# An FFN down projection on seven block products: one core, fp32 in three fp32r passes

## The reference, cut to what matters

```python
D_MODEL = 2048;  D_FF = 4 * D_MODEL;  SEQ = 512;  DEC_BATCH = 8   # 520 tokens reach the FFN
h = _rms_norm(x, g_ffn)
u = jnp.square(jax.nn.relu(jnp.einsum('bld,df->blf', h, w_up)))
return x + jnp.einsum('blf,fd->bld', u, w_down)
```

## Time and profile before

| what | us |
|---|---|
| median of three runs | 3292.89 |
| span of the profiled execution | 3293.0 |
| TensorE busy | 3158.8 (96%) |
| VectorE busy | 1949.6 (59%) |
| ScalarE busy | 1439.7 (44%) |
| first matmul of the up projection | at 1860.09 |
| last product of the up projection | at 2527.92 |
| last addition to xd | at 3287.26 |

### The profile page before, as it was taken

How to read it: one execution, slowest core, us unless ns; L and a number is a source line. 1 busy time by engine, 2 the same in 40 slices (tenths; PEclk the granted TensorE clock), 3 DMA queues, 4 the chain that set the end, 5 groups by cost and what they waited for, 6 DMA issues and landing times.

```text
span 3293.0 us, 66551 instructions
## 1 busy us (share of the span) xinstructions
PE 3158.8 (96%) x24759; PEld 3020.4 (92%) x24759; DVE 1949.6 (59%) x2700; ACT 1439.7 (44%) x1998; POOL 342.2 (10%) x623
## 2 busy tenths in 40 slices
PE   6999999999999999899889699999999999999999
PEld 6999999999999998775389699999999999999999
DVE  4225666665555558899843687887876333433333
ACT  4224666665555556677722344444443122121211
POOL 1111111111111113233300000000000000000000
PEclk9999999999999999999999899999999999999999
DMA  6434333333343338799953244444445323333322
GB/s 186 114 107 110 102 97 99 106 101 93 108 114 93 106 96 297 270 362 326 377 188 102 90 129 128 128 132 135 135 134 191 128 93 115 115 117 122 120 90 91
DMA packets 506127, 472.92 MB, mean 144 GB/s; under 512 B 19680, under 2 KB 435312, under 8 KB 504856
## 3 DMA queue, kind: packets, MB, share of 16 engines
q1 hardware_dynamic: 465616, 353.80, 36.1%
q0 software_dynamic: 40416, 117.93, 10.4%
HBM read 426.85 MB, written 44.80 MB: 143 GB/s over the span
## 4 chain that ended last, share of the span: by engine, by line
PE 88%; DVE 6%; DMA 3%; ACT 1%; issue 1%; POOL 0%; SPq 0%; POOLq 0%; ACTq 0%; DVEq 0%
PE ps L901 26%; PE ps L902 26%; PE ps L903 26%; PE ps L1084 3%; PE ps L1095 2%; PE ps L1096 2%; PE ps L1017 2%; DMA pg<-in_cache_fox_v_dram 1%; DVE pg_lo L1773 1%; PE ps L1127 1%; PE ps L1126 1%; PE ps L948 1%; DMA x2T<-xT_dram 0%; DVE qp_lo L1773 0%; DVE w_lo L1773 0%
## 5 line engine op out<-in xcount | busy, mean ns | idle before, releaser
L901 PE MATMUL ps<-h_hi,w_hi 128*128 128x260 f32 (+1 forms) x2592 | 750.0, 289 | 16.1 <-DVE h_lo L1773 13.0
L902 PE MATMUL ps<-h_hi,w_lo 128*128 128x260 f32 (+1 forms) x2592 | 737.3, 284 | 0.0
L903 PE MATMUL ps<-h_lo,w_hi 128*128 128x260 f32 (+1 forms) x2592 | 736.5, 284 | 0.0
L1773 DVE TENSOR_TENSOR w_lo<-w_raw,w_hi 128x2048 fp32r<-128x2048 f32 (+1 forms) x241 | 466.8, 1937 | 275.4 <-ACT w_hi L1323 239.6
L1323 ACT ACTIVATE w_hi<-w_raw 128x2048 fp32r<-128x2048 f32 x160 | 305.9, 1912 | 693.0 <-PE ps L903 680.1
L901 PE MATMUL ps<-ub_hi,w_hi 128*128 128x260 f32 x2048 | 581.6, 284 | 9.9 <-DVE xd L2184 5.5
L903 PE MATMUL ps<-ub_lo,w_hi 128*128 128x260 f32 x2048 | 580.4, 283 | 0.0
L902 PE MATMUL ps<-ub_hi,w_lo 128*128 128x260 f32 x2048 | 580.2, 283 | 0.0
L901 PE MATMUL ps<-b_hi,w_hi 128*128 128x260 f32 x1792 | 508.3, 284 | 29.6 <-DVE b_lo L1773 25.2
L901 PEld LDWEIGHTS ps<-h_hi,w_hi 128*128 128x128 f32 x2592 | 491.4, 190 | 19.6 <-DVE h_lo L1773 14.5
L902 PE MATMUL ps<-b_hi,w_lo 128*128 128x260 f32 x1792 | 508.3, 284 | 0.0
(11 more groups left out here) (303 smaller groups left out, 5160.4 us busy)
## 6 DMA issues: line engine op xcount, KB each, us to landing
w_raw<-in_w_in_dram SPq DMA_DIRECT2D x81, 1024.0 KB, 5.7
w_raw<-in_w_down_dram SPq DMA_DIRECT2D x64, 1024.0 KB, 5.4
w_raw<-in_w_up_dram SPq DMA_DIRECT2D x32, 1024.0 KB, 8.3
x2T<-in_w_up_dram SPq DMA_DIRECT2D x64, 512.0 KB, 5.4
pg<-in_cache_sb_v_dram POOLq DMA_DIRECT2D x106, 256.0 KB, 4.9
w_raw<-in_cache_fox_k_dram SPq DMA_DIRECT2D x72, 256.0 KB, 5.4
u_dram<-x2T SPq DMA_DIRECT2D x64, 260.0 KB, 3.0
u_st<-u_dram SPq DMA_DIRECT2D x8, 2080.0 KB, 7.8
```

The costliest lines, as they stand in the source:

```text
L901: pe.matmul(out, whi, xhi, start=first, stop=False, skip_group_check=more)
L902: pe.matmul(out, wlo, xhi, start=False, stop=False, skip_group_check=more)
L903: return pe.matmul(out, whi, xlo, start=False, stop=last, skip_group_check=more)
L1773: return dve.tensor_tensor(out, a, hi.bitcast(F32), ALU.subtract)
```

## The change

The down projection gets the same form as the up projection. NC becomes 4 chunks of KF = 8 pairs of u tiles (16 k-tiles); within a chunk there are 8 pairs (q) of output tiles, each with seven block products of 24 matmuls. Pairs are numbered through, 0 to 31 up and 32 to 63 down (`Pair`), and `weights`, `high`, `low`, `weight_sum` and `product` serve both.

- The seven token blocks of the down projection are no longer formed from u by itself: the up projection computes them per pair (u11, u21 and u22 themselves, and t5 = u12 - u11, t6 = u22 - t5, u22 - u12, t4 = u21 - t6: four more VectorE additions of 128x260 a pair), keeps them in u7 (two buffers in x2T), and POOL stores all seven slices (910 KB) to u_dram, which is now 7 x 128 x 32 x 260.
- At a chunk's end POOL loads block i (1040 KB, 8320 B a partition) into b_raw, which lies over b_lo, as soon as product i+1 of the chunk's last pair is done; ScalarE (`block_high`) and VectorE (`block_low`) split it in place. Blocks 0 to 3 are split within the last pair of a chunk, 4 to 6 within the first pair of the next.
- Weight blocks: a11, a12 and a21 have one buffer each now, in w_raw, and a22 two (one over the attention masks). SP loads each as 512 KB when the low part that reads it last is done.
- In the down projection VectorE adds the seven banks to xd (`add`, one of them to three quarters of the pair at once: 780 columns with the bank broadcast).
- xd lies where x2T was; SP loads tiles 0 to 3 early, POOL tiles 4 to 15 after the last store of u.
- The results are turned in place: `turn` (8 transposes of the pair before, into banks 6 and 7) and `turn_samples` (2) stand between the products of the last chunk's pairs, ScalarE copies back to xd, SP stores from there. yn goes.

The diff, cut to its core:

```diff
-S_WO, S_FF = 81, 97
-FC = 1024
-NC = FF // FC
+S_WO = 81
 NU = FF // (2 * P)
-KF = FC // P
+KF = 8
+NC = NU // KF
...
-        u_dram = nc.dram_tensor("u_dram", [FF // P, P, TQ], F32).ap()
+        u_dram = nc.dram_tensor("u_dram", [7, P, NU, HQ], F32).ap()
...
+        b_raw = at("b_raw", [P, 7, KT // 2, HQ], F32, HALF)
+        xd = at("xd", [P, KT, TQ], F32, at_r)
+        u7 = [x2T[:, 8:15, HQ * i:HQ * i + HQ] for i in range(2)]
+        u_p1, u_p16, u_p165 = (x2T[:, k, 0:HQ] for k in (7, 6, 5))
+        assert odd_at + 4096 <= late0
+        a22_odd = nc.alloc_sbuf_tensor_at("a22_odd", [P, KT // 2, P], F32, offset=odd_at)
+        a11, a12, a21 = w_raw[0][:, 0:8, :], w_raw[0][:, 8:16, :], w_raw[1][:, 0:8, :]
+        a22 = [w_raw[1][:, 8:16, :], a22_odd[:, :, :]]
...
+            def weights(g, b11, b12, b21, b22):
+
+                wait(sp, a_lo, count(g, 7, -7))
+                sp.dma_start(a22[g.p], b22).then_inc(a22_ld[g.p], 16)
+                wait(sp, a_lo, count(g, 7, -5))
+                sp.dma_start(a11, b11).then_inc(a11_ld, 16)
+                wait(sp, a_lo, count(g, 7, -2))
+                sp.dma_start(a21, b21).then_inc(a21_ld, 16)
+                wait(sp, a_lo, count(g, 7, -1))
+                sp.dma_start(a12, b12).then_inc(a12_ld, 16)
...
+            def store(g):
+                pool.wait_ge(r_ok, count(g, 2, 2))
+                pool.wait_ge(u_ok, count(g, 3, 3))
+                pool.wait_ge(t_ok, count(g, 4, 4))
+                dst = u_dram[:, :, g.n:g.n + 1, :] if not g.mult else u_dram[:, :, bass.ds(g.x * 2 + g.n, 1), :]
+                pool.dma_start(dst.rearrange("s p o t -> p s (o t)"), u7[g.p]).then_inc(u_sv[g.p], 16)
+
+            def block_load(g, c, i):
+
+                pool.wait_ge(p_ok, count(g, 7, i + 1))
+                src = u_dram[i, :, bass.ds(c * KF, KF), :] if not isinstance(c, int) else u_dram[i, :, c * KF:c * KF + KF, :]
+                pool.dma_start(b_raw[:, i, :, :], src).then_inc(blk_ld[i], 16)
+
+            for p in range(2):
+                store(Pair(p))
+            with pool.Fori(1, NU // 2 - 1) as j:
+                for p in range(2):
+                    store(Pair(p, j, 2))
+            pool.wait_ge(u_sv[0], 64)
+            pool.wait_ge(u_sv[1], 64)
+            for i in range(7):
+                block_load(Pair(NU - 1), 0, i)
+                if i == 0:
+                    store(Pair(NU - 2))
+            store(Pair(NU - 1))
+            pool.wait_ge(x2_sw, 16)
+            for p in range(2):
+                pool.wait_ge(u_sv[p], 8 * NU)
+            pool.dma_start(xd[:, 4:KT, :], x2_dram[:, 4:KT, :]).then_inc(xd_ld[1], 16)
+            with pool.Fori(0, NC - 1) as c:
+                for i in range(7):
+                    block_load(Pair(NU + KF - 1, c, KF), c + 1, i)
...
+            def down(g, fresh=None, turned=None):
+
+                a, b, c = g.p, 2 + g.p, 4 + g.p
+                if g.q == 1:
+                    pe.wait_ge(r_ok, 2 * NU)
+                    pe.wait_ge(c_ev, 5 * NU)
+                pe.wait_ge(e_ok, count(g, 7, -14 + 3))
+                product(g, 1, a, True, False, fresh)
+                pe.wait_ge(e_ok, count(g, 7, -14 + 6))
+                product(g, 6, b, True, False, fresh)
+                pe.wait_ge(e_ok, count(g, 7, 1))
+                product(g, 2, a, False, False, fresh)
+                if turned is not None:
+                    turn(turned)
+                pe.wait_ge(e_ok, count(g, 7, 2))
+                product(g, 5, b, False, False, fresh)
+                pe.wait_ge(e_ok, count(g, 7, -14 + 7))
+                product(g, 7, c, True, False, fresh)
+                if turned is not None:
+                    turn_samples(turned)
+                pe.wait_ge(e_ok, count(g, 7, 4))
+                product(g, 3, b, False, False, fresh)
+                pe.wait_ge(e_ok, count(g, 7, 5))
+                product(g, 4, c, False, False, fresh)
...
+            def block_high(c, i):
+                act.wait_ge(blk_ld[i], count(c, 16, 32))
+                act.activation(b_hi[:, i, :, :], b_raw[:, i, :, :], ACT.Copy).then_inc(blk_hi, 1)
...
+            def down(g, nxt, old=None, new=None, done=None):
+                high(g, 7)
+                if old is not None:
+                    block_high(old, 4)
+                high(g, 3)
+                if old is not None:
+                    block_high(old, 5)
+                if new is not None:
+                    block_high(new, 0)
+                high(g, 4)
+                if old is not None:
+                    block_high(old, 6)
+                if new is not None:
+                    block_high(new, 1)
+                if done is not None:
+                    turned(done)
                 if nxt is not None:
...
+                    high(nxt, 5)
+                    high(nxt, 1)
+                if new is not None:
+                    block_high(new, 2)
+                if done is not None:
+                    turned_samples(done)
+                if nxt is not None:
+                    high(nxt, 6)
+                if new is not None:
+                    block_high(new, 3)
+                if nxt is not None:
+                    high(nxt, 2)
+
...
+            def block_low(c, i):
+                dve.wait_ge(blk_hi, count(c, 7, i + BLK0 + 1))
+                minus(b_lo[:, i, :, :], b_raw[:, i, :, :], b_hi[:, i, :, :]).then_inc(blk_lo, 1)
...
                 low(g, 3)
-                if nxt is not None:
-                    first_sums(nxt)
+                low(g, 4)
+                weight_sum(nxt, 1)
                 dve.wait_ge(p_ok, count(g, 7, 4))
-                dve.tensor_tensor(u_p165[:, :], u_p1[:, :], b, ALU.add).then_inc(c_ev, 1)
-                low(g, 4)
-                if nxt is not None:
-                    low(nxt, 5)
-                    second_sum(nxt)
+                dve.tensor_tensor(u_p165, u_p1, b, ALU.add).then_inc(c_ev, 1)
+                if new is not None:
+                    block_low(new, 0)
+                weight_sum(nxt, 2)
+                low(nxt, 5)
                 dve.wait_ge(p_ok, count(g, 7, 5))
                 dve.wait_ge(c_ev, count(g, 5, 2))
-                wait(dve, u_sv[p], count((g[0], 0), 16, 0))
-                dve.tensor_tensor(u22, u_p165[:, :], c, ALU.add).then_inc(c_ev, 1)
+                wait(dve, u_sv[g.p], count2(g, 16, 0))
+                dve.tensor_tensor(u22, u_p165, c, ALU.add).then_inc(c_ev, 1)
+                low(nxt, 1)
+                relu_square(u22, 3)
+                if new is not None:
+                    block_low(new, 1)
+                weight_sum(nxt, 3)
+                dve.wait_ge(p_ok, count(g, 7, 6))
+                dve.tensor_tensor(u12, u_p1, b, ALU.add).then_inc(c_ev, 1)
+                low(nxt, 6)
+                relu_square(u12, 4)
+                dve.wait_ge(r_ok, count(g, 2, 2))
+                dve.wait_ge(u_ok, count(g, 3, 2))
+                dve.tensor_tensor(t5, u12, u11, ALU.subtract).then_inc(t_ok, 1)
+                if new is not None:
+                    block_low(new, 2)
+                dve.wait_ge(p_ok, count(g, 7, 7))
+                dve.tensor_tensor(u21, u_p16, c, ALU.add).then_inc(c_ev, 1)
+                dve.wait_ge(t_ok, count(g, 4, 1))
+                dve.tensor_tensor(t6, u22, t5, ALU.subtract).then_inc(t_ok, 1)
+                dve.tensor_tensor(u12, u22, u12, ALU.subtract).then_inc(t_ok, 1)
+                low(nxt, 2)
+                relu_square(u21, 5)
+                weight_sum(nxt, 4)
+                dve.wait_ge(u_ok, count(g, 3, 3))
+                dve.wait_ge(t_ok, count(g, 4, 2))
+                dve.tensor_tensor(t4, u21, t6, ALU.subtract).then_inc(t_ok, 1)
+                if new is not None:
+                    block_low(new, 3)
+
+            last = NU // 2 - 1
+            up(Pair(0), Pair(1), TOKENS[4:])
+            up(Pair(1), Pair(2))
+            with dve.Fori(1, last) as j:
+                up(Pair(0, j, 2), Pair(1, j, 2))
+                up(Pair(1, j, 2), Pair(2, j, 2))
+            up(Pair(NU - 2), Pair(NU - 1))
+            up(Pair(NU - 1), Pair(NU), (), Pair(0))

+            def down(g, nxt, old=None, new=None):
+                m = 2 * g.q
+                a, b, c = (ps[:, r + g.p, 0:HQ] for r in (0, 2, 4))
+                x11, x12, x21, x22 = (xd[:, m + i, h * HQ:(h + 1) * HQ] for i in range(2) for h in range(2))
+                x3 = xd[:, m:m + 2, :].rearrange("p m t -> p (m t)")[:, HQ:4 * HQ].rearrange("p (o t) -> p o t", o=3)
+
+                def add(n, x, bank, before=None):
+                    dve.wait_ge(p_ok, count(g, 7, n))
+                    if before is not None:
+                        dve.wait_ge(e_ok, count(g, 7, before))
+                    dve.tensor_tensor(x, x, bank, ALU.add).then_inc(e_ok, 1)
+
+                if g.q in (0, 2):
+                    dve.wait_ge(xd_ld[g.q // 2], 32 if g.q == 0 else 64)
```

(76 more changed lines are left out.)

461 lines of the change are left out of this document (158 added, 303 removed).

## The result

The changed kernel takes **3332.7 us** (median of 4 runs, 3323.82 to 3341.66) against 3292.98 for the kernel before on the same chip: a ratio of 1.012, 95% interval 1.0097 to 1.0143. It is slower by 40 us, where 3251 was forecast and 3280 was the top of the range. The profiled execution, from which all rows of this kernel come, is the longest of the four: 3341.66 us, span 3340.1. The four lie 18 us apart, those of the kernel before 5.

A forecast was written before the change was run, and what follows sets the result against it. TensorE, busy 96% of the span, was taken as the bound. From the 3293.0 us span, -94.4 - 13.8 - 2.5 + 15 + 37 + 17 = -41.7 gave 3251 us, range 3208 to 3280.

The forecast's parts named there:

- the ring: Up projection: VectorE's chain from first sum to low 7, 15.2 us plus a21's landing, costs nothing up to 4.9 us landing.
- -94.4: Down projection on TensorE: 6144 matmuls (737.9 us) become 5376 (643.5 us), saving 94.4 us.
- -13.8: Passage from up to down: the idle time and slow clock around the store-reload of the last u values go, saving 13.8 us.
- -2.5: Start of the up projection: TensorE's wait for eviction c2 shrinks as loads start earlier, saving 2.5 us, bounds 0 and -6.
- the fourth case: Up projection: VectorE saturates through more dependent waits, 1 us a pair, 3283 us; chance 0.20 together with the late-blocks rival.
- I take the median, 5.4: Up projection: a21 assumed to land in 5.4 us beside the store, costing 0.5 us x 31 pairs, +15 us.
- The third case: Up projection: a21 lands behind the store at 8.1 us, pairs take 23.3 us, 3335 us in all; chance 0.10.
- the ring in the down projection: Down projection: VectorE's chain closing on the a21 load takes 13.5 us, with no store beside it, so costs 0.
- The walk that gave 12.3 us: Chunk boundaries: stepping through late additions behind block work, TensorE loses 12.3 us at each of three boundaries.
- 37 + 17: Boundary costs: +37 us for three chunk boundaries, +17 us for the passage from up to down.
- The second case: Boundaries: blocks land late, boundaries 16.5 and passage 25 us, 3272 us, up to 3290 with late weights; chance 0.20 with VectorE saturation.
- the bare balance of 6.3 each: Chunk boundaries: VectorE's work over two pairs, 46.5 us against 40.2, a bare excess of 6.3 us.

The follow-up runs named there:

- late-stores version: Changed kernel, but POOL's store of a pair's seven slices waits until the a21 load two pairs ahead has landed: 3263.84 us.
- the gates on the weight loads: Late stores and reordered boundaries, plus block 1 sent only after a21 landed and block 2 only after a12: 3244.49 us.
- the new order: Late stores, plus block 0 rounded after high 4, later blocks one step later, block 3 in the next chunk, additions 4 and 5 earlier: 3255.71 us.
- the last three moves: On the gated version: a store behind all seven block loads, block 3 rounded before high 7, second pair's first sum before block 6's low part: 3235.95 us.
- experiment 2: Changed kernel, but at each boundary POOL sends the first token block only after the next pair's a21 landed: 3347.23 us.

## Why the prediction was wrong

**What held.** TensorE's part: 23991 matmuls, plain down pairs at 20.11 us, pairs with transposes at 21.2. At the late-stores version the whole sum can be read without the ring: 3293.0 - 94.4 - 13.8 - 2.5 + 88.2 = 3270.5, its span is 3268.5. So -94.4, -13.8 and the start are right together to 2 us. The end cost nothing: 5.9 us from the last addition to the end of the span, 5.7 before. The same version ends the fourth case: with the stores late, VectorE does the same work in every up pair and the pairs take 20.11. Two of the signs that the prediction named for being wrong are in the profile after: up pairs over 22 us (22.30), and waits of ScalarE for b_raw (25.4 us in 7).

**The step that failed first** is "I take the median, 5.4". It is the landing of a21 beside the store, and it was 6.8 in the median and 8.8 at most: +66 us in place of +15. The third case had the mechanism (the load lands beside the store, ring 15.2 us), its price (23.3 us a pair; measured 22.30) and the limit 6.9. It was put at 0.10 because "260 KB stores, two in a row, land in 3.0 us", so that bytes divided by a rate gave less than 7. That row is from a stage in which one queue worked alone; it says nothing about two. The runs show what a second queue does: 4.0 us without the store, up to 8.8 beside it, 17.8 beside five block loads whose packets were 7.4 KB against 0.5. By the Trainium skill (DMA: Bandwidth & Descriptors, Queues, rings and completion order) an engine takes a packet from each queue that has work in turn. The trace agrees in kind: near one packet for one from 2950 to 2956 (315 and 398), so that the small packets got 8% of the bytes. It does not show a fixed ratio, since from 2944 to 2950 it was 209 and 655, nor whether the profile counts as a packet what the page does.

**The step that failed next** is the ring in the down projection: "is shorter (13.5 us) and has no store: 0". It has no store, but at the boundaries it has seven block loads from the same POOL queue, sent at the moment a21 is sent. The walk that gave 12.3 us let block 0 land in 5.7 us and never asked when a21 would; the median block took 9.2 us. The boundaries cost 95.8 us together where 37 + 17 were forecast. The second case priced late blocks (16.5 and 25 us); for late weights it allowed "up to 3290" without working one through.

Two smaller slips did not decide. The steps listed for the ring add up to 14.8 us at the prediction's own prices, not 15.2 (the measured pair less the median landing is 15.5). And the fourth case, 3283, is called held in a range that ends at 3280.

The two failed steps added to the forecast: 3251.3 + 51 + 42 = 3344, against the 3340.1 of the span. Of the 4 us between them 1.4 are the first matmul of the up projection, at 1858.69 where it was at 1860.09; the rest was not followed up.

**What only the experiments showed.** That the boundaries have two causes and not one: the gates on the weight loads took 13.7 us of them (76.8 to 63.1), the new order took 11.4, and the last three moves, two of order and one in POOL's queue, another 6.4. Of the 56.7 us left, the bare balance of 6.3 each would be 25. What the other 32 consist of stays open.

## What to carry to other kernels

A load on which a one-buffer ring closes must be priced beside the transfers that leave at the same moment from other queues, with the size of their packets, and not by its median among its own kind. Write down for each such load what is sent within a few us of it; if the other transfer isn't urgent (here a store with a whole pair of slack), let it wait for the load: one wait gave 69 us. Where both are urgent, as at the chunk boundaries, a gate alone only turns the wait over to the other one (experiment 2); first take the urgent work out from behind it in each engine's order, then gate.

## What was not expected of the hardware

The load of 512 KB (512 B rows) took 4.0 us (median) in the up projection where no store left beside it, up to 8.8 beside one of 910 KB (1040 B rows), and 17.8 beside 1040 KB loads (8320 B rows), while the DMA engines together moved more than 400 GB/s in parts of that last stretch (423 from 2950 to 2956). The total rate was far from poor; the small packets' share of it was.
